# One decoder block on one core: GpSimd's table work released by another counter, one adaLN slab a place earlier, two transposes two steps earlier

## The reference, cut to what matters

```python
mods = c_act @ w_ada + b_ada                 # 9 vectors of 2048: shift, scale, gate of three blocks
x = x + 0.5 * g1 * swiglu(modulate(rms(x), sh1, sc1), w_ffn1_in, w_ffn1_out)
h = modulate(rms(x), sh2, sc2)
z, xbc, dt, u, gates = split(h @ w_in)
p_a = ssd_mixer(xbc, z, dt) @ w_a            # Mamba-2
p_b = glu(gelu(s5_mixer(u)) @ w_b_glu)       # diagonal complex SSM, 64 groups, 64 states each
x = x + g2 * ((sigmoid(gate_a) * p_a + sigmoid(gate_b) * p_b) @ w_out)
x = x + 0.5 * g3 * swiglu(modulate(rms(x), sh3, sc3), w_ffn2_in, w_ffn2_out)
out = rms_norm(x)
```

## Time and profile before

| what | value |
|---|---|
| median of 3 runs (lowest, highest) | 2449.39 us (2448.65, 2449.57) |
| profiled execution, its own time | 2448.65 us |
| its span | 2446.8 us |
| mean granted clock of TensorE | 0.989 |
| busy: TensorE, VectorE, ScalarE, GpSimd | 2371.2, 1747.5, 1052.2, 251.2 us |
| HBM read | 569.98 MB |

### The profile page before, as it was taken

How to read it: one execution, slowest core, us unless ns; L and a number is a source line. 1 busy time by engine, 2 the same in 40 slices (tenths; PEclk the granted TensorE clock), 3 DMA queues, 4 the chain that set the end, 5 groups by cost and what they waited for, 6 DMA issues and landing times.

```text
span 2446.8 us, 38205 instructions
## 1 busy us (share of the span) xinstructions
PE 2371.2 (97%) x15508; PEld 2120.5 (87%) x15508; DVE 1747.5 (71%) x2074; ACT 1052.2 (43%) x1134; POOL 251.2 (10%) x265
## 2 busy tenths in 40 slices
PE   6899999999999999999999999999999999999998
PEld 3478899888899999989899999998888888888987
DVE  3377787868778878888887786877776565444565
ACT  4243434343343454444355554334443454434444
POOL 1544133321320000000000000000000000000000
PEclk8999999999999999999999999999999999999999
DMA  9988877878778875555565467786687556555553
GB/s 359 386 270 295 286 263 265 303 269 295 273 256 290 303 261 173 173 183 178 174 237 191 147 219 258 273 314 238 243 297 287 168 185 200 190 187 178 194 185 112
DMA packets 296991, 584.60 MB, mean 239 GB/s; under 512 B 10324, under 2 KB 35412, under 8 KB 295316
## 3 DMA queue, kind: packets, MB, share of 16 engines
q1 hardware_dynamic: 291408, 559.98, 65.8%
q0 software_dynamic: 4144, 22.28, 2.5%
q10 hardware_dynamic: 1300, 0.35, 0.1%
HBM read 569.98 MB, written 12.58 MB: 238 GB/s over the span
## 4 chain that ended last, share of the span: by engine, by line
PE 82%; DVE 11%; DMA 3%; ACT 2%; issue 1%; POOL 0%; SPq 0%; ACTq 0%; DVEq 0%
PE gps L309 77%; DVE wlo L971 4%; PE mps L309 4%; DMA pre<-in_w_ada_dram 3%; DVE acc L989 1%; ACT whi L556 1%; DVE t L1552 1%; PE mps L1850 1%; DVE xz L1096 1%; DMA raw<-in_w_ffn_in_dram 0%; DVE wr L1563 0%; DVE wi L1558 0%; DVE t L1559 0%; DVE wr L1554 0%; DVE xw L1241 0%
## 5 line engine op out<-in xcount | busy, mean ns | idle before, releaser
L971 DVE TENSOR_TENSOR wlo<-raw,whi 128x1024 fp32r<-128x1024 f32 x800 | 986.8, 1275 | 493.0 <-ACT whi L556 490.9
L556 ACT ACTIVATE whi<-raw 128x1024 fp32r<-128x1024 f32 x800 | 803.4, 1052 | 1166.6 <-PE gps L309 1152.6
L309 PE MATMUL gps<-whi,hs 128*128 128x512 f32 (+1 forms) x2816 | 872.9, 388 | 10.9 <-DVE wlo L971 6.3
L309 PEld LDWEIGHTS gps<-whi,hs 128*128 128x128 f32 x2816 | 529.0, 188 | 131.8 <-issue 21.1
L309 PE MATMUL gps<-hs,whi 128*128 128x256 f32 x3072 | 569.0, 287 | 23.0 <-DVE wlo L971 18.4
L309 PE MATMUL gps<-wlo,hs 128*128 128x512 f32 (+1 forms) x1408 | 542.8, 386 | 0.0
L309 PEld LDWEIGHTS gps<-hs,whi 128*128 128x128 f32 x3072 | 484.9, 194 | 35.1 <-DVE wlo L971 20.9
L309 PE MATMUL gps<-ffs,whi 128*128 128x256 f32 (+1 forms) x2064 | 491.8, 322 | 2.5 <-DVE wlo L971 2.4
L309 PE MATMUL gps<-hs,wlo 128*128 128x256 f32 x1536 | 437.8, 285 | 0.0
L309 PE MATMUL gps<-ffs,wlo 128*128 128x256 f32 x1376 | 386.5, 281 | 0.0
L309 PEld LDWEIGHTS gps<-ffs,whi 128*128 128x128 f32 x2064 | 343.8, 190 | 34.5 <-DVE wlo L971 3.4
(11 more groups left out here) (279 smaller groups left out, 1396.6 us busy)
## 6 DMA issues: line engine op xcount, KB each, us to landing
raw<-in_w_ffn_in_dram SPq DMA_DIRECT2D x160, 1024.0 KB
raw<-in_w_ada_dram SPq DMA_DIRECT2D x112, 1024.0 KB
raw<-in_w_in_dram SPq DMA_DIRECT2D x80, 1024.0 KB
raw<-in_w_ffn_out_dram SPq DMA_DIRECT2D x56, 1024.0 KB
pre<-in_w_ada_dram SPq DMA_DIRECT2D x32, 1024.0 KB, 14.4
raw<-in_w_ffn_out_dram SPq DMA_DIRECT2D x40, 768.0 KB
raw<-in_w_b_glu_dram SPq DMA_DIRECT2D x32, 512.0 KB
raw<-in_w_a_proj_dram SPq DMA_DIRECT2D x16, 1024.0 KB
```

The lines of the kernel that those rows point to most:

```text
L309: return pe.matmul(out, lhsT, rhs, start=start, stop=stop, skip_group_check=True)
L556: act.activation(whi[:, mpos % SPLIT, h, :], raw[:, pos % RING, h, :], ACT.Copy).then_inc(hi_ready, 1)
L971: ins = dve.tensor_tensor(wlo[:, mpos % SPLIT, h, :], raw[:, pos % RING, h, :], whi[:, mpos % SPLIT, h, :].bitcast(F32), ALU.subtract)
```

## The change

Three edits.

1. In a phase whose groups have six slabs, the fourth ada slab follows the fourth slab of the second group and not the fifth. For four and for two slabs a group the new formula gives the places that the old list gave.
2. GpSimd's tables wait for `ada_done`, the count of finished chunks of `mods`, and no longer for `raw_used`. Table n waits for 10 + (12 n // 16), the first one too, which had no wait: 10, 10, 11, 12, 13, 13, 14, 15, 16, 16, 17, 18, 19, 19, 20, 21. Counted as chunks behind the prologue (0, 1, ...), table n waits for chunk 1, 1, 2, 3, 4, 4, 5, 6, 7, 7, 8, 9, 10, 10, 11, 12; before it was none, 0, 0, 1, 2, 3, 3, 4, 4, 5, 6, 7, 8, 9, 10, 10.
3. In the u phase TensorE's first two transposes come at step 12 and not 14; all later steps stay where they were.

```diff
-                places.setdefault(n + {6: (0, 1, 2, 4), 4: (0, 1, 2, 3), 2: (0, 0, 1, 1)}[n][t], []).append(("ada", 0, t))
+                places.setdefault(n + (t if n >= 4 else t // 2), []).append(("ada", 0, t))
...
-            chunk_summed, count = [], 0
-            for kind, ph in steps:
-                if kind == "gemm":
-                    for _ in range(ph.bodies):
-                        chunk_summed += [count + pos + 1 for pos, (what, _, s) in enumerate(ph.stream)
-                                         if what == "ada" and s == 3]
-                        count += len(ph.stream)
             for n in range(2 * UT):
-                if n:
-                    pool.wait_ge(raw_used, chunk_summed[(0, 0, 1, 2, 3, 3, 4, 4, 5, 6, 7, 8, 9, 10, 10)[n - 1]])
+                pool.wait_ge(sem("ada_done"), 10 + n * 12 // 16)
                 if n >= 2:
...
-                yield from steps_of_u(13)
+                yield from steps_of_u(11)
                 turns(0)
-                yield from steps_of_u(2)
+                yield from steps_of_u(4)
                 pe.wait_ge(sem("wdt_lo"), 1)
```

## The result

| | before | after |
|---|---|---|
| median, same chip (lowest, highest) | 2449.02 us (2448.02, 2449.57), 4 runs | 2466.4 us (2463.49, 2469.4), 4 runs |
| profiled execution, own time | 2448.65 | 2468.89 |
| its span | 2446.8 | 2467.1 |
| mean granted clock | 0.989 | 0.986 |

The ratio is 1.0072, 95% interval 1.0058 to 1.0084: 17.4 us slower. The prediction was 2463.4 with a range of 2453 to 2470, and the measured time lies in that range.

What follows compares the result with a forecast made beforehand. The prediction took TensorE's matmuls (82% of the chain) as the bound. Its terms summed to +14.4 us on the profiled 2448.65, giving 2463.05; with half the offset to the median it said 2463.4, range 2453 to 2470.

Steps and rivals of the forecast that it cites:

- GpSimd yields: Rival, all table places: GpSimd waits behind VectorE's queued work instead of delaying it; -2.3 us, 2446, chance 0.05.
- accumulations are not slowed: Rival, all table places: tables don't stretch VectorE's accumulations (line 989); +4.3 us, 2453, chance 0.13.
- First pair body: Table 0 leaves this body, so TensorE's wait behind stretched VectorE pairs and a late slab goes: 1.4 us gained.
- Doubles in pair bodies: Tables 0, 1 and 8, 9 start with a chunk's sum; the second of each delays TensorE 2.0 us, 4.0 together.
- First output phase, tables and stream: Wait at 337.36 mostly goes (-0.6), tables 4 and 5 cost 1.2, the earlier chunk slab 1.0 over both bodies.
- Narrow phase: Tables 12 and 13 replace 14 and 15 beside narrow matmuls: same total, 0, with -1.5 to +1.5 us.
- Table 14: Second output phase, behind the sum at 751.49: five to six table operations delay a busy VectorE; TensorE waits 4.7 us.
- Table 15: Released by the sum at 778.62: three to four table operations delay VectorE, slack 1.9; cost 1.3 us (0.3 to 2.0).
- Transposes: U phase: TensorE reaches the first transposes two tiles earlier and waits for VectorE's blocks; cost 2.5 us (2.0 to 2.6).
- clock: One half-clock stretch follows the new TensorE waits over 2 us outside the pair bodies: 1.7 us (0 to 5).
- late-ring rival: Rival: VectorE's delay frees slabs later, so slab DMAs land late at doubles and table 14; 2470 us, chance 0.15.
- if only the lo pairs were slowed: Case where tables stretch only VectorE's low-half slab operations, not accumulations: the sum would be 8.1 us lower.

Runs made afterwards that it cites:

- e6: Changed kernel with the six operations of each table only writing (memsets): 2446.31 us against 2450.34 of the kernel before and 2468.55 of the changed kernel.
- e2: Kernel before with edit 2 alone (tables released by ada_done): 2459.73 us against 2450.99, ratio 1.0040.
- e5: e4 with the second of each two tables waiting for the body's first low half: 2442.23 us against 2450.34 of the kernel before, ratio 0.9965.
- e7: The changed kernel run again without an edit, on another chip: 2468.55 us against 2450.34 of the kernel before, ratio 1.0069.
- e8: Kernel before with the first transposes one step earlier instead of two: 2450.02 us, one run.
- e10: e4 with each table's first and fourth operation also waited for by the next: 2442.05 us against 2451.86 of the kernel before, ratio 0.9962.
- e1: Kernel before with edit 1 alone (fourth ada slab one place earlier in the first output phase): 2453.39 us against 2450.99, ratio 1.0009.
- e3: Kernel before with edit 3 alone (first transposes two steps earlier): 2451.68 us against 2450.99, ratio 1.0006.
- e4: Kernel before with the same 16 tables at other chunks, mostly two back to back in pair bodies: 2447.88 us against 2450.99, ratio 0.9988.
- e9: e5 with its last table moved behind chunk 11's sum: 2446.75 us against 2451.86 of the kernel before, ratio 0.9984.

## Why the prediction was right, and where its terms were off

*The direction and the mechanism.* Right: GpSimd's table operations and VectorE's operations on SBUF tiles hold each other up, and the new places are those where TensorE is due on VectorE. e6 shows it, where the tables only write and nothing is stretched; the rivals "GpSimd yields" and "accumulations are not slowed" fall with e2 and with the rows at 254.11 and 760.74. The Trainium skill (SBUF — State Buffer, Who interferes with whom) says that a VectorE instruction with two SBUF inputs contends with a GpSimd instruction that reads SBUF and not with one that only writes; the runs agree with both halves, 4.60 us for three accumulations beside reads, 2.33 beside writes or nothing.

*First pair body: -1.4.* The wait is gone, and e2's profile gains 2.0. In the profile after the gain is used up: TensorE's first matmul of this stage started at 137.76 instead of 136.00, behind a half-clock stretch at 122.4 in the prologue that the profile of before lacks, and at chunk 0 the two are level. That stretch comes and goes: the profiles of e5, e7, e8 and e10 have one there too, those of e1, e2, e3, e4, e6 and e9 don't. It is scatter of the prologue, not the change.

*Doubles in pair bodies: +4.0, measured 7.0 (5.6 in the profiles of e7, the same kernel, and of e2).* This is the term that was mis-sized most. The step that failed is "VectorE meets four to five table operations, 0.98 us each", as one wait. Two operations pass back to back without letting VectorE in, so the first lo pair (5.36 us) is already late for TensorE (1.3 us), and then the next one again (1.8 us). e10 shows it at e4's places: with a semaphore between those two operations the extra all but disappears. (The changed kernel wasn't run with it.) Whether the first of the two waits comes hangs on little: after, the lo pair starts 0.1 us behind the second table (247.51 against 247.40). In e7's first double it starts 1.8 us behind it (247.92 against 246.11), takes 3.66 us, and only the second wait is left. The single tables 2 and 11 cost 0.5 each besides, which I had at nothing.

*First output phase, tables and stream: -0.6 + 1.2 + 1.0 = +1.6, measured 0.7.* The wait at 337.36 went (0.8 us), slab 10's of 0.9 us came in both bodies as worked out, slab 11's of 0.4 us went in both, and there are two waits (401, 411) beside tables 4 and 5, 0.75 us each, where 1.2 was said in all. What the sum didn't have: the wait of 0.64 us for slab 9 of the second body (427.13 before) is gone as well, behind these two.

*Narrow phase: 0, measured 0.0*, with 0.5 for table 11 ahead of it. Instead of one wait of 3.0 us there are three (0.6, 1.3, 0.9).

*Table 14: 4.7, measured 3.6.* I let each of five to six table operations cost 0.98 us. Three accumulations lost 2.27 us, 0.76 each, the lo pair 1.72, and the first accumulation (760.22) nothing: 4.0 us less the slack of 0.7, so 3.3. So the idle time is under the 4 us that the profile after was to show. *Table 15: 1.3, measured 1.9*: the additions of squares (two SBUF inputs as well) were left out of the sum. The chain of the kernel after has them:

```profile
799.20 1.48 DVE sq L1073
...
800.70 1.41 DVE sq L1074
```

where the two took 1.1 us together before.

*Transposes: 2.5, measured 2.4* in e3 and *clock: 1.7, measured about 3.7*: 1.6 behind table 14 (5.2 - 3.6) and 2.1 in the u phase (4.5 - 2.4). The forecast counted one stretch and three came in new or longer. Its price for one was a little high: 18 matmuls instead of 28 are 10 x 0.1207 = 1.2 us and not 1.7, and stretches of 3.4 us cost 1.4 us (e3) to 1.6 us (e1, and behind table 14). The late-ring rival was half right: ScalarE's idle time that ends with a slab's landing grows from 10.5 us (2 times) to 35.9 (8 times), near 268 and 575 behind the doubles above all, but TensorE doesn't stand behind any of them. e5 has 41.8 us of it (12 times) and is 26 us faster than the changed kernel. The ring got late and it cost nothing.

Sum: 0 + 7.0 + 0.9 + 0.7 + 0 + 3.6 + 1.9 + 2.4 + 3.7 = 20.2 against 20.2. The mis-sizings of both signs, +3.0 for the doubles, +2.0 for the clock, +1.4 for the prologue's scatter, -1.1 for table 14 and -0.9 for the output phase, make up most of the 5.8 us by which this profile is over the sum of 14.4; against the medians, 17.4, the sum was 3 us low. That it came so near is in part luck, since misses of both signs cancelled.

One figure of the prediction doesn't agree with its own rival: if only the lo pairs were slowed, the terms that it lists there (4.0, 3.4, 1.0 and the clock's 1.7) take 10.1 us off, not 8.1. Nothing else was worked out from the 8.1.

## What to carry to other kernels

Side work on GpSimd that nobody waits for still has a price, and it is set by what VectorE is doing at that time: place it by VectorE's slack, not by its own due time. Two operations queued on GpSimd without a wait between them blocked VectorE as one of double length when VectorE's came due just as they started; with e10's two waits, or with e5's later start, the same work cost TensorE next to nothing at places with slack. And where a kernel runs matmuls end to end, read a small edit's cost from an instruction in the trace that comes once per chunk, because the clock's stretches elsewhere move a run's time by as much.

## What was not expected of the hardware

A half-clock stretch follows an idle stretch of TensorE only sometimes: behind the same 3.7 us from start to start (table 14's place) it was 3.4 us long in the profiles of the changed kernel and of e2, 6.8 in e7's, and absent in e9's. Behind 2.26 us from start to start near 980 to 1000 it came in six of the twelve profiles (before, after, e1, e5, e7, e8) and not in the other six (e2, e3, e4, e6, e9, e10). Over the 29 runs of before beside e1 to e4, those with a mean clock of 0.985 took 2454.7 and 2455.0 us and those with 0.990 took 2448.5 to 2450.3. What decides it stays open.
